# Chunk states of the recurrent heads: from GpSimd pairs to fused VectorE steps placed after the selection rounds

## The reference, cut to what matters

```python
def _hgrn2_mixer(q, f_raw, v, lb):
    f = lbh + (1.0 - lbh) * jax.nn.sigmoid(f_raw)
    k = 1.0 - f
    bc = jnp.cumsum(chunkify(jnp.log(f)), axis=3)
    def step(state, inp):
        qn, kn, vn, bn = inp
        diff = bn[:, :, :, None, :] - bn[:, :, None, :, :]
        decay = jnp.exp(jnp.where(causal[:, :, None], diff, -jnp.inf))
        scores = jnp.einsum('bhtk,bhsk,bhtsk->bhts', qn, kn, decay)
        o = (jnp.einsum('bhts,bhsv->bhtv', scores, vn)
             + jnp.einsum('bhtk,bhkv->bhtv', qn * jnp.exp(bn), state))
        b_last = bn[:, :, -1:, :]
        state = (jnp.exp(b_last[:, :, 0, :])[..., None] * state
                 + jnp.einsum('bhsk,bhsv->bhkv', kn * jnp.exp(b_last - bn), vn))
        return state, o
```

## Time and profile before

| | |
|---|---|
| Median of three runs | 1521.97 us (1519.91, 1521.97, 1523.24) |
| The profiled execution's own time | 1523.21 us |
| Its span, first to last instruction | 1521.9 us |
| Mean granted TensorE clock | 0.997 |
| PE busy | 1502.0 us, 99% |
| DVE busy | 984.1 us, 65% |
| ACT busy | 664.4 us, 44% |
| POOL busy | 171.3 us, 11% |

### The profile page before, as it was taken

The page is one execution under the profiler, slowest core; times in us unless marked ns, Lnnn a source line. Parts: engine busy times, 40 slices in busy tenths (PEclk is TensorE's granted clock), DMA queues, the critical chain, the costliest instruction groups (busy, mean ns, idle before and its releaser), DMA issues.

```text
span 1521.9 us, 18695 instructions
## 1 busy us (share of the span) xinstructions
PE 1502.0 (99%) x7390; PEld 1228.6 (81%) x7390; DVE 984.1 (65%) x1607; ACT 664.4 (44%) x1133; POOL 171.3 (11%) x180
## 2 busy tenths in 40 slices
PE   8999999999999999999999999999999999999998
PEld 6788878888888888877777978888888876778786
DVE  7677667966666564877776743434444549979774
ACT  6455444513233233555565532413233446555660
POOL 0000002000000002111111100000000202776200
PEclk9999999999999999999999999999999999999999
DMA  9334444565655543122212343333333221212131
GB/s 370 128 133 159 137 137 161 177 211 193 195 192 195 193 153 115 42 83 70 68 58 80 96 123 97 97 97 97 97 97 97 78 90 66 75 50 73 39 111 56
DMA packets 52554, 182.09 MB, mean 120 GB/s; under 512 B 5825, under 2 KB 6721, under 8 KB 52466
## 3 DMA queue, kind: packets, MB, share of 16 engines
q1 hardware_dynamic: 52466, 180.90, 36.1%
HBM read 177.33 MB, written 3.41 MB: 119 GB/s over the span
## 4 chain that ended last, share of the span: by engine, by line
PE 89%; DVE 6%; ACT 2%; POOL 2%; issue 1%; DMA 0%; SPq 0%; DVEq 0%; ACTq 0%
PE PS L534 23%; PE PS L537 23%; PE PS L535 23%; PE PS L600 2%; PE PS L781 1%; PE PS L800 1%; PE PS L545 1%; PE PS L547 1%; PE PS L544 1%; DVE sb_Wl L1726 1%; POOL sb_TMD L2432 1%; PE PS L1097 1%; PE PS L1091 1%; PE PS L1092 1%; PE PS L619 1%
## 5 line engine op out<-in xcount | busy, mean ns | idle before, releaser
L534 PE MATMUL PS<-sb_Hh,sb_Wh 128*128 128x512 f32 (+1 forms) x1016 | 406.1, 400 | 2.2 <-DVE sb_Hl L1757 2.2
L537 PE MATMUL PS<-sb_Hh,sb_Wl 128*128 128x512 f32 (+1 forms) x1016 | 397.1, 391 | 0.6 <-DVE sb_Wl L1726 0.6
L535 PE MATMUL PS<-sb_Hl,sb_Wh 128*128 128x512 f32 (+1 forms) x1016 | 397.0, 391 | 0.0
L1141 ACT ACTIVATE sb_Wh<-sb_RAW 128x1024 fp32r<-128x1024 f32 (+1 forms) x218 | 228.6, 1049 | 287.4 <-PE PS L537 280.6
L1726 DVE TENSOR_TENSOR sb_Wl<-sb_RAW,sb_Wh 128x1024 fp32r<-128x1024 f32 (+1 forms) x218 | 268.3, 1232 | 71.1 <-ACT sb_Wh L1141 70.9
L534 PE MATMUL PS<-sb_Oh,sb_Wh 128*128 128x512 f32 x600 | 235.4, 392 | 0.4 <-ACT sb_rg L1326 0.4
L534 PEld LDWEIGHTS PS<-sb_Hh,sb_Wh 128*128 128x128 f32 (+1 forms) x1016 | 190.6, 188 | 56.0 <-issue 12.9
L537 PE MATMUL PS<-sb_Oh,sb_Wl 128*128 128x512 f32 x600 | 233.9, 390 | 0.0
L535 PE MATMUL PS<-sb_Ol,sb_Wh 128*128 128x512 f32 x600 | 233.7, 390 | 0.0
L537 PEld LDWEIGHTS PS<-sb_Hh,sb_Wl 128*128 128x128 f32 (+1 forms) x1016 | 190.4, 187 | 42.6 <-DVE sb_Wl L1726 1.0
L535 PEld LDWEIGHTS PS<-sb_Hl,sb_Wh 128*128 128x128 f32 (+1 forms) x1016 | 190.6, 188 | 39.9 <-issue 1.2
(11 more groups left out here) (413 smaller groups left out, 2035.6 us busy)
## 6 DMA issues: line engine op xcount, KB each, us to landing
sb_RAW<-w SPq DMA_DIRECT2D x128, 512.0 KB, 3.6
sb_ARW<-ada SPq DMA_DIRECT2D x86, 512.0 KB, 4.4
sb_RAW<-diff_in SPq DMA_DIRECT2D x24, 512.0 KB, 3.6
sb_RAW<-gla_in SPq DMA_DIRECT2D x20, 512.0 KB, 3.6
sb_RAW<-in_b SPq DMA_DIRECT2D x16, 512.0 KB, 3.7
sb_RAW<-gla_wo SPq DMA_DIRECT2D x8, 512.0 KB, 3.5
sb_RAW<-diff_wo SPq DMA_DIRECT2D x8, 512.0 KB, 3.5
sb_RAW<-wo SPq DMA_DIRECT2D x8, 512.0 KB, 3.6
```

Of the source, the lines that this page charges most:

```text
L534: mm(to[0:m, :], WH[si][:, k, 0:m], hi[:, k, :], start=first, stop=False)
L535: mm(to[0:m, :], WH[si][:, k, 0:m], lo[:, k, :], start=False, stop=False)
L537: ins = mm(to[0:m, :], WL[si][:, k, 0:m], hi[:, k, :], start=False, stop=last)
L1141: act(WH[slot_of(b)][:, :, 0:m], RAWS[raw_of(b)][:, 0:8 * m].rearrange("p (k m) -> p k m", k=8), ACT.Copy).then_inc(*done("w_hi", b))
```

## The change

On DVE, a new helper `states(n)` stands at the end of each tick, behind `w_next` and the selection rounds for the ticks before 26, and directly behind `two_tick(n)` for ticks from 26 on. When step 7 of a recurrent head is due, it issues six `scalar_tensor_tensor` instructions of 128x128, S2[m] = S2[m-1] * dec[m] + S2[m], each waiting for the one before. POOL's step 7, with its twelve instructions and its scratch tile, goes. On POOL, in steps 2 and 3 the differences of the next two levels stand ahead of the multiplications of the present two. PE's, ACT's and SP's programs are unchanged. Lines behind L2311 move down: the former L2396, L2397, L2404, L2420, L2425 are L2408, L2409, L2416, L2432, L2437, and the new instruction is L2319.

```diff
+            def states(n):
+                for kind, h, step in due(TWO_TASKS, n):
+                    if kind == "rec" and step == 7:
+                        e.wait_ge(at("r_copy", h, 1), at("r_dec", h))
+                        for m in range(1, 7):
+                            if m > 1:
+                                e.wait_ge(at("r_state", h, m - 1))
+                            stt(S2[:, m, :], S2[:, m - 1, :], dec[:, h, m:m + 1], S2[:, m, :], ALU.mult,
+                                ALU.add).then_inc(*done("r_state", h, m))
...
                     w_next(b)
                 for i, r in TOP.get(n, ()):
                     top(i, r)
+                states(n)
             for n in range(TICK_FIRST, 31):
                 two_tick(n)
+                states(n)
                 if n < 29:
                     w_next(TWO + n - 1)
                     one_more(TWO + n, ORDER_2[n])
...
                 elif step == 2:
+                    from_middle(h, 2, 3)
                     decayed(h, 0, 1)
-                    from_middle(h, 2, 3)
                 elif step == 3:
+                    from_middle(h, 4, 5)
                     decayed(h, 2, 3)
-                    from_middle(h, 4, 5)
...
-                elif step == 7:
-                    d, free = TP.take(("ds", h), ("r_state", h, 6))
-                    e.wait_ge(at("r_copy", h, 1), at("r_dec", h), *free)
-                    for n in range(1, 7):
-                        if n > 1:
-                            e.wait_ge(at("r_state", h, n - 1))
-                        e.op.tensor_scalar(d[:, 0:128], S2[:, n - 1, :], dec[:, h, n:n + 1], None,
-                                           ALU.mult).then_inc(*done("r_ds", h, n))
-                        e.wait_ge(at("r_ds", h, n))
-                        tt(S2[:, n, :], d[:, 0:128], S2[:, n, :], ALU.add).then_inc(*done("r_state", h, n))
```

## The result

The changed kernel takes 1538.67 us (median of 4 runs, 1536.48 to 1541.35), against 1522.61 for the kernel before, measured beside it (1519.91 to 1523.75). The ratio is 1.0101, with a 95% interval of 1.0086 to 1.0115: slower by about 1%. Two more sets of five runs gave 1538.45 us (ratio 1.0101) and 1540.23 us (1.0105). The forecast was 1535.5 us with a full range from 1528 to 1542; of its own narrower range, 1533 to 1538, the three medians lie 0.5 to 2.2 us above the upper end.

The account below looks back on a forecast made before the run. PE, busy 99% of the span, was taken as the bound. Late states 13.8, L932's waits -0.8, relief -1.2 and clock +1.7 made 13.5 us on the 1521.97 median: 1535.5 us, own range 1533 to 1538, full 1528 to 1542.

Parts of the forecast that it names:

- the clock costs more: Rival: PE's low-clock stretches cover only work and come again at head 3; 3 to 4 us more, 1539; chance 0.15.
- Chain of a head: DVE's six fused states come every 0.385 us; the sixth is ready 2.28 us after DVE begins.
- Late states less L932's waits and the relief: PE's last state products later by 13.8 us over four heads, minus 0.8 for L932's waits on POOL, minus 1.2 relief.
- PE's last state product starts 0.06 us after its state is ready: At each head's output on PE: the gap from sixth state to last product, 0.06 us, taken from the kernel before.
- Clock: PE's clock behind the outputs: one new low stretch behind head 2, heads 0 and 1 as before; +1.7 us, 0 to 5.
- Relief: DVE's instructions run faster with 48 POOL instructions gone from beside them; -1.2 us, ends 0 and 3.
- The rival with 4.5 us more: Rival: DVE's two-input instructions speed up more without POOL, states of heads 0 to 2 start sooner; 1531; chance 0.17.
- The reordering: POOL's earlier differences cost nothing, covered by POOL's slack; if that failed, at most 1 us a head.
- PE stops waiting: Rival: the fused chain is done before PE's outputs ask and the clock stays high; 8.1 us faster, 1513.9; chance 0.05.

Follow-up runs that it names:

- e3: The changed kernel with the six fused states per head moved to the front of every DVE tick; 1517.58 us, ratio 0.9965 to the kernel before.
- e4: The changed kernel with the states moved ahead of the selection rounds, still behind merges and weight block; 1522.29 us, ratio 0.9993 to the kernel before.
- e10: The kernel before, with POOL's states of heads 0 to 2 held until DVE's selection rounds end; 1554.89 us, ratio 1.0206 to the kernel before.
- e12: The changed kernel with POOL's old order, differences behind the present multiplications, run again; 1539.68 us, ratio 1.0109 to the kernel before.

## Why the prediction was right, and where it was off

The mechanism held, and e3, e4 and e10 show it from three sides; the time it takes was mis-sized in two terms. The rounds and the mask stand ahead of the states, PE's output asks before DVE gets there, and DVE doesn't catch up between the heads. The side, slower, was given 0.92. The size is right only by the full range: 1538.67 us is 0.7 above the forecast's own range, and nearest to the 1539 of "the clock costs more". Term by term, against the profiled pair:

- **Chain of a head.** Worked out as 2.28 us; measured 2.28 in all four heads.
- **Late states less L932's waits and the relief.** 13.8 - 0.8 - 1.2 = 11.8 us worked out, 15.2 measured (3.7, 3.5, 7.0 and 1.0 by head). The step that failed is "PE's last state product starts 0.06 us after its state is ready", carried over from the kernel before. From DVE's begin to PE's next work the prediction makes 2.28 + 0.06 + 0.70 - 0.27 = 2.8 us at head 0. Head 3, at a clock of 1.00, takes 1449.63 - 1447.02 = 2.61, where the same sum with its shorter last step makes some 2.5. Heads 0, 1 and 2 take 3.87, 3.83 and 3.87: behind the halt PE runs at 1.2 GHz, and its own products for a chunk then take (1333.69 - 1332.41)/2 = 0.64 us, more than DVE's 0.385 us a state, where they took (1329.78 - 1329.11)/2 = 0.34 before. That is some 1.1 us a head, 3.3 in all, and nearly the whole difference of 3.4. In the kernel before this could not be seen, since the clock was 1.00 over all four outputs, and POOL's pairs, 1.25 us apart, were slower than PE at either clock.
- **Clock.** +1.7 worked out for a new low stretch behind head 2, with the two behind heads 0 and 1 unchanged. The times between one output's end and the next output's first product changed by -0.9, -0.2 and +0.9 us, together -0.2. The granted clock over these three pieces was 0.93, 0.95 and 1.00 and is now 0.95, 0.94 and 0.97. So the new low stretch behind head 2 came, at about 1 us; the one behind head 0 shrank, which accounts for some 0.6 of the 0.9 us there, and the one behind head 1 stayed. Inside the outputs of heads 0, 1 and 2 the clock was 1.00 and is now 0.70, 0.79 and 0.63. The prediction put the clock's price behind the outputs only, and the larger part of what is new fell inside them. The two misses hang together, and the sum of both is 15.0 us against 13.5.
- **Relief.** Taken as 1.2 us. The low half ahead of head 1's states took 1.19 us where it took 1.42, that ahead of head 2's 1.22 instead of 1.47, and the mask instruction 0.43 instead of 0.86: 0.9 us. At head 0 the low half took the same (1.22 and 1.21), but L2296 ahead of it 0.68 instead of 0.94. Set against PE's first product of the head, DVE's begin lies 0.7 us earlier than worked out at head 0, 0.5 later at head 1, 0.9 and 0.1 earlier at heads 2 and 3: 1.2 us in all, as the term had it. The rival with 4.5 us more did not come. The Trainium skill's rule on the two engines (SBUF — State Buffer, Who interferes with whom) is not refuted by that: in the changed kernel the states simply don't meet POOL. In e3 they do, at head 1, and take 3.85 us instead of 2.28, one instruction up to 717 ns against a median of 352; there the trace agrees with the rule.
- **The reordering.** Costed at nothing, and inside the change that stands, within some 2 us. Where those could come from the prediction missed: not POOL's own time, but DVE's L2191, 0.9 us shorter without the differences beside it. Its cover was misnamed as well: it is not POOL's slack but the absence of the states. Without that, 2.3 us at heads 1 and 2 and not "at most 1 us".

The terms measured make 15.2 - 0.2 = 15.0 us, and the spans differ by 13.2. The rest lies ahead of the change's place. ACT's conversion L1141 waits for a weight transfer, and the wait differs from trace to trace. In the kernel before:

```profile
1290.86 1.06 ACT L1141 ACTIVATE sb_Wh<-sb_RAW 128x1024 fp32r<-128x1024 f32 x1 [2.92 <-DMA sb_RAW<-in_b]
```

In the changed one:

```profile
1290.11 1.06 ACT L1141 ACTIVATE sb_Wh<-sb_RAW 128x1024 fp32r<-128x1024 f32 x1 [1.78 <-DMA sb_RAW<-in_b]
```

The changed kernel's profiled execution reached head 0's output 1.7 us early (1326.79 against 1328.45). The early landing is part of that, and luck; but e12, with a wait as short (1.93 us) and POOL's old order, gained nothing by it, so the new order has a part in it too. The medians are 15 to 17 us apart. So the forecast was 1.2 to 3.3 us short; 1.5 of that is the low clock inside the outputs (3.3) less what the clock term had too much (1.7 against -0.2), and what is left is within the spread of the runs.

Of the rivals, "PE stops waiting" did not happen in the change, and its point of decision was named rightly: with the rounds out of the way (e3), its 8.1 us were there at head 2 (8.2). What it lacked is that DVE becomes the bound and hands 2.6 back. "The clock costs more" (1539, chance 0.15) comes nearest by its number, and half of its mechanism came: low stretches that cover only work, 3.3 us inside three outputs. The other half, one more at head 3, did not: the clock there is 1.00. By the Trainium skill (GPSIMD Engine Reference, Engine selection) elementwise work belongs on VectorE; per instruction the trace agrees (0.35 us against 0.60 + 0.46), and e3 gains by it. The change itself loses 1% with the same instruction. The measurement decides: which engine does the work counted for less here than what stands ahead of it in that engine's queue.

## What to carry to other kernels

Before a job moves to a faster engine, read in that engine's timeline when it would begin, and set that against the moment the consumer asks; here a chain that is 6 to 7 us shorter but begins 8 to 12.5 us later, measured against that moment, loses. In a queue worked strictly in order, put what another engine waits for ahead of what nobody waits for: here the same 24 instructions are worth 21 us between the two places. An order of instructions that is harmless together with an edit can cost 7 us without it, so halves of a change are to be priced apart.

## What the runs showed of the hardware

A halt of PE is dearer than its length where the work behind it is a chain of small products: the clock is down to 1.2 GHz at the latest with the first products behind halts of 3.4 to 6.4 us, and the output's products take 0.95 us for four instead of 0.56, about 1.1 us a head on top of the waiting. Fused VectorE steps of 128x128 that wait for one another come every 0.385 us, and took 3.85 instead of 2.28 us for six when GpSimd's 128x256 operations ran beside them; likewise two VectorE multiplications of 128x256 took 1.64 instead of 0.75 us. The wait for one weight transfer near 1290 us lay between 1.6 and 3.5 us in the traces of these kernels. With the new order PE's next level products moved with it by up to 2 us; with the old order they came late in every trace. Why that transfer lands so differently was not looked into.
